# Fourteen instead of nine convolution taps summed by accumulating transfers, and three modulation sums at other turns

## What is computed

```python
mod = (silu(c) @ w_mod + b_mod)[:, None, :]
sh1, sc1, g1, sh2, sc2, g2 = jnp.split(mod, 6, axis=-1)
h = rms_norm(x, norm1_g) * (1.0 + sc1) + sh1
z = h @ w_in          # FoX q,k,v,forget | NSA q,k,v,gates | convolution a, gate
mixed = concatenate([o_fox, o_nsa, o_conv], axis=-1)
x = x + g1 * (mixed @ w_out)
h = rms_norm(x, norm2_g) * (1.0 + sc2) + sh2
x = x + g2 * (square(relu(h @ w_mlp1)) @ w_mlp2)
out = rms_norm(x, final_g)
```

## Time and profile before

| | |
|---|---|
| median of 3 runs | 1186.9 us (1186.18 to 1186.96) |
| the profiled execution, its own time | 1185.15 us |
| its span | 1183.1 us |
| PE busy | 1139.2 us (96%) |
| DVE busy | 989.9 us (84%) |
| ACT busy | 638.0 us (54%) |
| POOL busy | 23.5 us (2%) |
| mean DMA rate | 266 GB/s |
| convolution products on ACT | 183 to 293 us |
| FoX attention | about 236 to 306 us |
| NSA attention | about 312 to 425 us |

### The profile page before, as it was taken

How to read it: one execution, slowest core, us unless ns; L and a number is a source line. 1 busy time by engine, 2 the same in 40 slices (tenths; PEclk the granted TensorE clock), 3 DMA queues, 4 the chain that set the end, 5 groups by cost and what they waited for, 6 DMA issues and landing times.

```text
span 1183.1 us, 17839 instructions
## 1 busy us (share of the span) xinstructions
PE 1139.2 (96%) x7081; PEld 1007.9 (85%) x7081; DVE 989.9 (84%) x1197; ACT 638.0 (54%) x929; POOL 23.5 (2%) x40
## 2 busy tenths in 40 slices
PE   4998999999999998999999999999999999999996
PEld 4898989998877777999788888888888888888885
DVE  5998989989889988996887787987788987778675
ACT  6655448877664546445544445544445554445452
POOL 2000000100000000001000000000000000000000
PEclk7999999999999999999999999999999999999998
DMA  9999998878957897995657676566675657766451
GB/s 375 421 420 420 420 379 308 264 197 297 310 207 256 290 309 268 380 384 181 209 186 266 236 276 208 183 213 249 250 265 196 208 188 273 257 217 260 162 178 71
DMA packets 48322, 314.65 MB, mean 266 GB/s; under 512 B 6572, under 2 KB 8440, under 8 KB 11768
## 3 DMA queue, kind: packets, MB, share of 16 engines
q1 hardware_dynamic: 44592, 305.72, 69.9%
q0 software_dynamic: 1760, 5.26, 2.3%
q10 hardware_dynamic: 1896, 2.64, 0.8%
HBM read 305.20 MB, written 4.21 MB: 262 GB/s over the span
## 4 chain that ended last, share of the span: by engine, by line
PE 75%; DVE 11%; DMA 6%; ACT 4%; issue 4%; SPq 0%; ACTq 0%; DVEq 0%
PE quad L1249 15%; PE quad L1263 10%; PE quad L1265 10%; PE quad L1264 10%; PE quad L1251 8%; PE quad L1239 5%; PE quad L1241 5%; PE quad L1240 5%; DMA mod_raw<-in_w_mod 3%; DMA first_raw<-in_w_mod 2%; DVE w_lo L1796 2%; DVE mod_raw L1803 2%; PE quad L1310 2%; PE quad L1311 2%; PE quad L1309 2%
## 5 line engine op out<-in xcount | busy, mean ns | idle before, releaser
L870 ACT ACTIVATE w_hi<-raw 128x1024 fp32r<-128x1024 f32 (+1 forms) x342 | 355.4, 1044 | 312.2 <-PE quad L1265 119.9
L1796 DVE TENSOR_TENSOR w_lo<-raw,w_hi 128x1024 fp32r<-128x1024 f32 (+1 forms) x342 | 408.6, 1205 | 116.3 <-ACT w_hi L870 114.5
L1249 PE MATMUL quad<-act,w_hi 128*128 128x512 f32 x768 | 266.4, 390 | 0.0
L1239 PE MATMUL quad<-act,w_hi 128*128 128x256 f32 x760 | 215.8, 284 | 7.3 <-DVE w_lo L1796 5.2
L1251 PE MATMUL quad<-act,w_lo 128*128 128x256 f32 x768 | 216.6, 282 | 0.0
L1240 PE MATMUL quad<-act,w_hi 128*128 128x256 f32 x760 | 213.7, 281 | 0.0
L1241 PE MATMUL quad<-act,w_lo 128*128 128x256 f32 x760 | 213.5, 281 | 0.0
L1249 PEld LDWEIGHTS quad<-act,w_hi 128*128 128x128 f32 x768 | 144.2, 188 | 30.1
L1239 PEld LDWEIGHTS quad<-act,w_hi 128*128 128x128 f32 x760 | 144.5, 190 | 10.0 <-issue 7.2
L1263 PE MATMUL quad<-w_hi,u_hi 128*128 128x512 f32 x376 | 148.9, 396 | 0.6 <-DVE u_lo L2266 0.6
L1265 PE MATMUL quad<-w_hi,u_lo 128*128 128x512 f32 x376 | 148.8, 396 | 0.0
(11 more groups left out here) (367 smaller groups left out, 1712.5 us busy)
## 6 DMA issues: line engine op xcount, KB each, us to landing
raw<-in_w_main SPq DMA_DIRECT2D x184, 1024.0 KB, 5.1
mod_raw<-in_w_mod SPq DMA_DIRECT2D x72, 1024.0 KB, 7.1
first_raw<-in_w_mod SPq DMA_DIRECT2D x14, 1024.0 KB, 14.7
late_raw<-in_w_mod SPq DMA_DIRECT2D x10, 1024.0 KB, 8.2
conv_b<-conv_q POOLq DMA_DIRECT2D x8, 512.0 KB, 5.9
x_a<-in_x SPq DMA_DIRECT2D x2, 1024.0 KB, 7.1
x_scratch<-x SPq DMA_DIRECT2D x1, 2048.0 KB, 12.8
x<-x_scratch SPq DMA_DIRECT2D x1, 2048.0 KB, 10.6
```

Of the source, the lines that this page charges most:

```text
L870: A(dst[:, 0:2 * width], block_half(raw, j, width), ACT.Copy).then_inc(hi_done, 1)
L1239: mm(out, hi, act_hi[:, k, :], start=begin and m % 2 == 0, stop=False, skip_group_check=True)
L1249: mm(out, w_hi[j % 4][:, cols], act_both[:, k, :, :].rearrange("p h t -> p (h t)"), start=begin, stop=False, skip_group_check=True)
L1796: TTn(lo[:, 0:2 * width], block_half(raw, j, width), hi[:, 0:2 * width].bitcast(f32), ALU.subtract)\
```

## The change

Every odd tap from 1 to 27 goes to an accumulating transfer, 14 taps in place of 9, and the chain on DVE loses five adds: 14 scalar taps are left (0, 2, 4, 6, 8, 10, 12, 14, 16, 20, 24, 28, 29, 30), 13 of which are added. The transfers' products alternate between `conv_q` and `conv_p[1]`. That leaves the scalar taps only `conv_p[0]`, except tap 29 (`SPARE_TAP`), which takes `conv_p[1]` once the transfers before the last are done. So ACT's product of a scalar tap waits for the add of the scalar tap right before it (two before, for tap 30), and the product of the n-th transfer waits for transfer n - 2. Of the modulation sums, those of turns 81, 95 and 96 are taken out of the table, and turns 62, 65 and 68 have one each. Sums keep their order, so sum 39 is now at turn 62, 40 at 65, 41 at 68, 42 at 76, and so on up to 47 at turn 86; from turn 99 on the table is the same.

```diff
-DMA_TAPS = [2, 5, 8, 11, 14, 17, 20, 23, 27]
+DMA_TAPS = list(range(1, CONV_W - 3, 2))
 CHAIN_TAPS = [tap for tap in range(CONV_W) if tap not in DMA_TAPS]
 SCALAR_TAPS = [tap for tap in CHAIN_TAPS if tap not in VECTOR_TAPS]
+SPARE_TAP = CONV_W - 2
...
-MODS_AT |= {FOX_AT + AHEAD + t: 1 for t in (1, 3, 5, 6, 7, 9, 11)}
-MODS_AT |= {NSA_TURN + t: 1 for t in (0, 1, 4, 7, 9, 13, 14, 15, 17, 18, 19, 20, 21, 23)}
+MODS_AT |= {turn: 1 for turn in (62, 65, 68)}
+MODS_AT |= {FOX_AT + AHEAD + t: 1 for t in (1, 3, 5, 7, 9, 11)}
+MODS_AT |= {NSA_TURN + t: 1 for t in (4, 7, 9, 13, 14, 15, 17, 18, 19, 20, 21, 23)}
...
+        def tap_buffer(n):
+
+            return conv_b if n == 0 else conv_q if n % 2 else conv_p[1]
...
-                    pool.dma_start(conv_b[:, :, :], conv_q[:, :, :], accum_op=ALU.add).then_inc(tap_sum, 16)
+                    pool.dma_start(conv_b[:, :, :], tap_buffer(n)[:, :, :], accum_op=ALU.add).then_inc(tap_sum, 16)
...
-                    if n > 1:
-                        act.wait_ge(tap_sum, 16 * (n - 1))
+                    if n > 2:
+                        act.wait_ge(tap_sum, 16 * (n - 2))
                     for ct in range(CT):
-                        last = A((conv_q if n else conv_b)[:, ct, :], conv_in[:, ct, tap:tap + S], ACT.Copy,
+                        last = A(tap_buffer(n)[:, ct, :], conv_in[:, ct, tap:tap + S], ACT.Copy,
                                  scale=convw[:, ct, tap:tap + 1])
...
-                    act.wait_ge(conv_sem, CHAIN_TAPS.index(SCALAR_TAPS[i - 2]) + 1 if i > 2 else 1)
+                    act.wait_ge(conv_sem, CHAIN_TAPS.index(SCALAR_TAPS[i - (2 if tap > SPARE_TAP else 1)]) + 1
+                                if i > 1 and tap != SPARE_TAP else 1)
+                    if tap == SPARE_TAP:
+                        act.wait_ge(tap_sum, 16 * (len(DMA_TAPS) - 2))
                     for ct in range(CT):
-                        dst = conv_y[:, ct, :] if tap == 0 else conv_p[i % 2][:, ct, :]
+                        dst = conv_y[:, ct, :] if tap == 0 else conv_p[tap == SPARE_TAP][:, ct, :]
...
-                    TTn(conv_y[:, :, :], conv_y[:, :, :], conv_p[n % 2][:, :, :], ALU.add).then_inc(conv_sem, 1)
+                    TTn(conv_y[:, :, :], conv_y[:, :, :], conv_p[tap == SPARE_TAP][:, :, :], ALU.add).then_inc(conv_sem, 1)
```

## The result

| | before | after |
|---|---|---|
| median of 5 runs | 1186.96 us (1186.18 to 1188.45) | 1196.33 us (1193.82 to 1203.26) |
| ratio, 95% interval | | 1.0091 [1.0073, 1.0109] |
| the profiled execution, its span | 1185.15, 1183.1 us | 1203.26, 1201.5 us |

The change makes the kernel slower by 9.4 us. The forecast was 1187.2 us, and its range ended at 1191.6: both were wrong. Note the spread: the runs of after lie within 9.4 us of each other, those of before within 2.3. The profiled execution is the slowest of the five, so its waits are those of a bad case.

The account below looks back on a forecast made before the run. The prediction took PE to bound the kernel, busy for 1139.2 of 1183.1 us. Its terms, -0.8 + 2.0 + 2.4 - 3.3 = +0.3, added to 1186.9 gave 1187.2 us, with a range from 1182.8 to 1191.6.

Parts of the forecast that it names:

- The transfers: Convolution: 13 chained transfers two turns (5.6 us) apart, landing in 6.3 us each; ACT never waits where it counts.
- 0.7 a tap: Convolution up to turn 75: how far the chain slips per tap at 6.3 us a landing, in us.
- POOL waits for ACT at each of them: Issue of the transfers: the reason why POOL's 5 more issues were to cost nothing.
- Rival 2: Convolution, tap 17 at turn 73: the chain falls behind, first scores 4.4 us later, 1191.6 us; chance 0.26.
- Place A: PE's wait before half 61: DVE's gate chain starts sooner, wait shrinks from 1.42 to about 0.6 us; -0.8 us.
- Place B: Halves 68 and 69: moved sums eat DVE's lead, PE waits for `w_lo`; +2.0 us, some 0.3 at half 68.
- Place C: First scores, turn 75: one shared product buffer delays ACT's casts, then DVE's scores; +2.4 us for two waits.
- Place D: Four FoX waits of PE, turns 77 to 83: they go as sums and adds ahead are removed; -3.3 us.
- I cost their removal at nothing: Turns 95 and 96: taking their two sums away was to gain nothing, as DVE waits for PE there anyway.
- From NSA turn 3 on, stretches are as long as before: NSA attention: an expected sign that the change leaves the time there as it was.
- The sum: Whole kernel: -0.8 + 2.0 + 2.4 - 3.3 = +0.3 us, giving 1187.2 us; chance 0.40.
- the ledger: The prediction's list of gains and losses at four places, from the half 61 wait to the FoX waits; +0.3 us.

Follow-up runs that it names:

- short transfers: The changed kernel with 128 KB instead of 512 KB in each accumulating transfer, the other three channel tiles' sum left out: 1187.48 us, ratio 1.0015.
- the taps alone: The changed kernel with its fourteen taps by transfer, but the modulation sums where the kernel before had them: 1196.82 us, ratio 1.0113.
- the dense chain: The changed kernel's fourteen transfers, with modulation sums at turns 73 and 93 instead of 62, 65 and 68: 1190.24 us, ratio 1.0031.

## Why the prediction was wrong

- **The transfers, "6.3 each ... ACT ... never waits in the stretch where it counts": this step failed.** The median landing was 8.1 us, and the first four took 9.3 us from issue to issue. Two mistakes lie in it. I took the duration from a chain with mostly three turns between transfers and, from 205 to 245 us, no sum loads beside it, and did not let the transfers fall where other loads run: the first came 5.5 us earlier and took 9.8 us instead of 4.6, with the moved sums and (10.0) without them. And I left out the gap between a landing and the next issue, about 0.5 us: a chain's period is landing plus gap, so 5.6 us a tap could only hold landings under 5.1, and the old median was already 5.9. I saw the slip of "0.7 a tap" and trusted two buffers to hold it. "POOL waits for ACT at each of them" failed with it: POOL waited for a landing at twelve of its thirteen issues. The loads "share the queues with the chain" is loosely put: the page of the profile lists them on queues of their own, and what they share is the 16 DMA engines.
- **Rival 2 was the mechanism**, with a chance of 0.26 and a price of 4.4 us. Both were too small: at landings of 8.1 us, near the 8.3 that it was priced for, the loss was 9.4 us and not 4.7 (0.3 + 4.4). Its place was too late as well: I looked at tap 17 and the sixth transfer alone, but tap 11 at turn 67 wants the third in the same way. ACT came to it at 221.86 - 3.47 = 218.4, and the landing was at 221.77. In the profiled execution the price is higher since four waits of ACT (11.8 us) come before the first scores, and since PE comes back from its own longest wait at 1.2 GHz: half 73 then took 4.45 us where it had taken 3.05. How the median's 9.4 us divides between waits and clock is not shown.
- **Place A** held: a wait of 0.57 us (0.53 with short transfers) against "about 0.6".
- **Place B** held where the chain is out of the way: 1.59 us before half 69 against 2.0 with 0.3 of it at half 68. In the changed kernel it stands at 230.57, mixed with the chain's delay.
- **Place C** was a little high: 1.54 and 0.33 us for the two waits against 2.4.
- **Place D** held in the FoX turns: the four waits are gone in the changed kernel too, and PE makes up 3.9 us between halves 74 and 81. But some of it came back in the NSA turns. There "I cost their removal at nothing" and "From NSA turn 3 on, stretches are as long as before" failed: in the run with short transfers PE waits 3.00, 0.68 and 0.45 us in place of 1.41, 1.35 and 0.81, +0.6 us. PE waits for DVE there, so whatever DVE does earlier or later moves it.
- **The sum** of the four places, +0.3 us, compares with +1.8 us [0.6, 2.9] of the run with short transfers (0.0015 x 1186.1 and its interval), or +0.7 of its profiled execution over before's 1185.15. With 0.6 for the NSA turns the ledger comes to +0.9, right to about a microsecond, partly by luck, as its errors have both signs. It was a ledger of VectorE, and what decided was the chain.

The Trainium skill, "DMA: Bandwidth & Descriptors", section "Two DMAs through the same engine are not ordered", asks that the issuing engine wait for the first DMA's semaphore before it issues a dependent one; that wait is what makes each landing count in full here, and the trace agrees in POOL's rows. Its estimate of 3.2 us for one transfer (section "Anatomy of one DMA — SWDGE (gpsimd) path"), by which the chain could never be late, is further off than it looked: the least of the changed kernel is 5.7 us. What one landing in this chain costs alone, with no load beside it, was not measured.

## What to carry to other kernels

A chain of dependent transfers has a period, landing plus reissue, and that period, taken under the load which the change itself creates, must be shorter than the spacing of the consumers; a median from a sparser chain is no evidence, and a buffer or two of lead only delays the first wait. Look at who shares an engine's queue with the product that waits: here the casts did, so a transfer that saved 1.13 us of VectorE could stop TensorE for 5. Moving three sums and exchanging one tap, with the chain left as sparse as it was, gave 0.5%. A wait that is taken away can come back in part where the engine is late next (0.8 of 2 us here), until that place is relieved too.

## What was not expected of the hardware

- The landing of a chained accumulating transfer grows far less than its size: medians of 5.0, 5.7 and 6.7 to 8.1 us for 128, 256 and 512 KB, while single ones of 512 KB ranged from 4.5 to 12.2 us. In the kernel before, those of 4.5 to 4.8 us ran while the core moved 143 to 190 GB/s, and the one of 11.7 us at 312 GB/s, beside weight and modulation loads.
- A few microseconds without matmuls can cost more than themselves: after waits of 4.95 and 6.17 us, matmuls of 256 columns stood 0.21 us apart instead of 0.12 for 3 and 4.5 us, and even a wait of 2.33 us, in the run with the taps alone, was followed by a window at 0.75. In the kernel before the clock fell at about 343 us with no such wait ahead of it.
- The same program with the dense chain took from 1180.35 to 1197.5 us, where before's runs differ by 2 to 4 us.
